# Router logits with tokens on partitions, and their place among the projection's last matmuls

## The reference, cut to what matters

```
h  = h + (y * g) @ w_o                       # layer 0's mixer; layer 1: silu(u) @ w_pw2 + b
ht = rms_norm(h, norm2_g)
gp = softmax(ht @ w_group + b_group)         # 4 groups
p_top, g_idx = top_k(gp, 1)
el = ht @ w_expert + b_expert                # 32 experts, 8 a group
el_sel = the 8 of el in the chosen group
top_l, e_idx = top_k(el_sel, 2)
gates = softmax(top_l) * p_top               # for the two experts that a token chose
h  = h + sum over experts of gate * (silu(ht @ wg) * (ht @ wu)) @ wd
```

## Time and profile before

| | us |
|---|---|
| median of 3 runs | 1217.81 |
| lowest and highest | 1216.09, 1220.73 |
| time of the profiled execution | 1218.87 |
| its span in the profile | 1217.1 |
| PE busy in that span | 1144.6 (94%) |
| DVE busy | 529.2 (43%) |
| ACT busy | 425.1 (35%) |
| mean granted clock of PE | 0.991 of 2.4 GHz |

### The profile page before, as it was taken

How to read it: one execution, slowest core, us unless ns; L and a number is a source line. 1 busy time by engine, 2 the same in 40 slices (tenths; PEclk the granted TensorE clock), 3 DMA queues, 4 the chain that set the end, 5 groups by cost and what they waited for, 6 DMA issues and landing times.

```text
span 1217.1 us, 29462 instructions
## 1 busy us (share of the span) xinstructions
PE 1144.6 (94%) x12520; PEld 627.2 (52%) x12520; DVE 529.2 (43%) x1004; ACT 425.1 (35%) x823; POOL 205.6 (17%) x234
## 2 busy tenths in 40 slices
PE   6999999999999989999998889999999999998785
PEld 5365555555555644555554445544554555554442
DVE  6756464664555510511111125899941511111125
ACT  5345354454454421321121124555443321111123
POOL 2000000000000000222222110688800112221110
PEclk9999999999999999999999999999999999999998
DMA  4017311011011258799999998126702889999996
GB/s 162 3 55 297 116 56 41 20 59 42 20 59 49 98 201 339 283 354 421 423 420 423 424 379 344 70 71 253 316 1 75 324 304 422 422 423 422 422 401 256
DMA packets 53779, 281.97 MB, mean 232 GB/s; under 512 B 14956, under 2 KB 17132, under 8 KB 36496
## 3 DMA queue, kind: packets, MB, share of 16 engines
q1 hardware_dynamic: 43952, 263.73, 54.1%
q0 software_dynamic: 9408, 16.32, 3.7%
q10 hardware_dynamic: 288, 0.03, 0.0%
HBM read 265.84 MB, written 30.41 MB: 243 GB/s over the span
## 4 chain that ended last, share of the span: by engine, by line
PE 79%; DMA 12%; DVE 3%; ACT 2%; issue 2%; SPq 1%; DVEq 0%; ACTq 0%
PE psum L1609 15%; PE psum L974 14%; PE psum L2143 9%; PE psum L2441 8%; PE psum L1790 6%; PE psum L987 6%; DMA h<-rows 5%; DMA big<-in_moe_w_gate_up_dram 4%; DMA h<-in_moe_w_gate_up_dram 4%; PE psum L941 2%; PE psum L1914 1%; PE psum L1779 1%; SPq L423 1%; PE psum L2451 1%; PE psum L2417 1%
## 5 line engine op out<-in xcount | busy, mean ns | idle before, releaser
L974 PE MATMUL psum<-big 128*64 128x256 f32 x1536 | 188.4, 388 | 24.0 <-issue 13.2
L1609 PE MATMUL psum<-big 128*128 128x512 f32 x384 | 192.8, 623 | 1.4 <-ACT big L1660 0.2
L974 PEld LDWEIGHTS psum<-big 128*64 128x64 f32 x1536 | 107.0, 138 | 92.2 <-issue 33.1
L1108 DVE SCALAR_TENSOR_TENSOR big<-psum,big 128x128 f32<-128x128 f32 x64 | 22.4, 351 | 292.2 <-ACT big L1058 292.2
L987 PE MATMUL psum<-big 128*64 128x512 f32 x512 | 121.0, 593 | 1.1 <-DMA big<-in_moe_w_down_dram 0.8
L2143 PE MATMUL psum<-big 128*128 128x512 f32 x256 | 115.6, 604 | 0.8 <-ACT big L2544 0.8
L894 POOL DMA_INDIRECT chosen<-big x60 | 59.9, 998 | 312.3 <-ACT big L1069 150.7
L1983 ACT COPY big<-psum 128x512 f32<-128x512 f32 (+1 forms) x112 | 69.1, 649 | 109.8 <-PE psum L1790 107.4
L2386 POOL TENSOR_TENSOR big<-big 128x512 f32<-128x512 f32 x76 | 96.7, 1272 | 36.0 <-ACT big L2526 25.5
L1790 PEld LDWEIGHTS psum<-big 64*64 64x64 f32 x4096 | 71.5, 134 | 49.3 <-issue 48.5
L2441 PE MATMUL psum<-big,conv_w 128*128 128x512 f32 x224 | 96.5, 592 | 0.0
(11 more groups left out here) (290 smaller groups left out, 1395.2 us busy)
## 6 DMA issues: line engine op xcount, KB each, us to landing
big<-in_moe_w_gate_up_dram SPq DMA_DIRECT2D x40, 2048.0 KB, 31.1
big<-in_moe_w_down_dram SPq DMA_DIRECT2D x64, 1024.0 KB, 27.7
conv_w<-in_moe_w_gate_up_dram SPq DMA_DIRECT2D x8, 2048.0 KB, 31.6
h<-in_moe_w_gate_up_dram SPq DMA_DIRECT2D x8, 2048.0 KB, 26.6
big<-in_moe_w_gate_up_dram SPq DMA_DIRECT2D x16, 1024.0 KB, 12.3
big<-in_rwkv_w_rkv_dram SPq DMA_DIRECT2D x24, 512.0 KB, 4.2
chosen<-h SPq DMA_DIRECT2D x8, 1024.0 KB, 12.6
conv_w<-in_conv_w_pw_dram SPq DMA_DIRECT2D x8, 1024.0 KB, 4.8
```

The costliest lines, as they stand in the source:

```text
L974: last = nc.tensor.matmul(o[half * SLOTS:(half + 1) * SLOTS, 0:F_EXP].rearrange("p (u f) -> p u f", u=2), m.xT[e // 2 % 2][:, c, (e % 2) * ...
L1609: last = nc.tensor.matmul(bank[b], m.w[:, n, c, :], x[:, c, :], start=(c == 0), stop=(c == C - 1))
```

## The change

The logits' operands change places: 128 tokens of hnT are the stationary operand and the 36 columns of the table stream past. So logits come out with tokens on partitions, and both copies and the second turning are gone. Each tile has matmuls of its own: 8 calls a tile, 32 in all, as before.

PE makes the logits of tiles 0 and 1 inside the projection, behind chunk 3 of tile 3, and turns tile 2 ahead of tile 3's last chunk. Behind the projection stay the logits of tile 2, the turning of tile 3 and the logits of tile 3. DVE chooses tiles 0 and 1 as a pair while the projection runs, then tile 2 alone and tile 3 alone; picks and token codes are made with each choice, and the two conversions of indices to float are gone. ACT codes tiles 0 and 1 early, and fills its zeros (L631) only behind all logits. `pe_stay_busy` ahead of the ranks goes from 5 matmuls to 2. PSUM banks are dealt out anew.

```diff
-        NORM_BANKS = ((6, 7), (2, 3)) * 2
+        OPENING_NORM_BANKS = ((6, 7), (2, 3)) * 2
+        NORM_BANKS = ((6, 7), (2, 3), (2, 3), (0, 1))
...
-        FLIP_BANKS = (4, 6, 5, 7)
+        LOGIT_BANK = (6, 7, 2, 0)
...
+        def pe_logits(m, pe, t):
+
+            if t == 0:
+                pe.wait_ge(m.router_scaled.sem, m.router_scaled.by(1))
             for c in range(C):
...
+                if c in (0, C // 2):
+                    pe.wait_ge(m.hnT_ready.sem, m.hnT_ready.by(2 * t + (1 if c == 0 else 2)))
+                last = nc.tensor.matmul(bank[LOGIT_BANK[t]][:, 0:N_LOGITS], m.hnT[:, c, t * P:(t + 1) * P],
+                                        m.w_route[:, c, :], start=(c == 0), stop=(c == C - 1))
+            last.then_inc(m.logits_in_psum.sem, 1)
+
+        def pe_route_last(m, pe):
+
+            pe_logits(m, pe, TT - 2)
             pe_norm_columns(m, pe, TT - 1)
-            pe_flip_logits(m, mixer, pe, 0)
-            pe_logits(m, mixer, pe, 1)
-            pe_flip_logits(m, mixer, pe, 1)
+            pe_logits(m, pe, TT - 1)
...
             for t in range(2):
                 square(t)
                 root(t)
-            columns(0)
-            square(2)
-            root(2)
-            columns(1)
-            columns(2)
-            square(3)
-            logits(0)
-            logits(1)
-            root(3)
-            columns(3)
-            logits(2)
+            for t in range(2):
+                columns(t)
+            act_low_codes(m, act, 0, 2)
+            for t in range(2, TT):
+                square(t)
+                columns(t)
+                root(t)
             act.wait_ge(m.squares.sem, m.squares.by(TT))
+            act.wait_ge(m.logits_in_psum.sem, m.logits_in_psum.by(TT))
...
+            dve_mixed(mixer, dve, 1)
+            dve_mean_square(m, dve, 1)
+            dve.wait_ge(consts_ready, 2)
+            step(nc.vector.memset(m.logits[:, :, n:], -3.0e38))
+            choose_experts(0, 2)
+            dve_mixed(mixer, dve, 2)
+            dve_mean_square(m, dve, 2)
+            dve_mixed(mixer, dve, 3)
+            choose_experts(2, 3, meanwhile=lambda: dve_mean_square(m, dve, 3))
+            choose_experts(3, 4)
...
-            pe_stay_busy(m, 5)
-            pe.wait_ge(m.route, PICKED)
+            pe_stay_busy(m, 2)
+            pe.wait_ge(m.route, PICKED[TT])
...
+        LOGITS_BEHIND = 3
...
                     for c in group:
                         add(t, c)
+                        if t == TT - 1 and c == LOGITS_BEHIND:
+                            for u in range(2):
+                                pe_logits(after, pe, u)
+                        if t == TT - 1 and c == C - 2:
+                            pe_norm_columns(after, pe, 2)
```

More of the change, by code:

```diff
@@ L561, in pe_logits @@
             for c in range(C):
[L562 to L576, removed]
@@ L669, in choose_experts @@
                 step(last)
-                for t in two:
+                for t in range(first, end):
                     last = nc.vector.max(m.gmax[:, t, :], m.logits[:, t, N_EXP:])
                 step(last)
-                for t in two:
+                for t in range(first, end):
                     last = nc.vector.max_index(m.gidx[:, t, :].bitcast(u32), m.gmax[:, t, :], m.logits[:, t, N_EXP:])
                 step(last)
-                step(nc.vector.tensor_copy(m.gidx_f[:, both], m.gidx[:, both, 0].bitcast(u32)))
@@ L685, in choose_experts @@
-                for t in two:
+                step(nc.vector.tensor_tensor(m.in_group[:, tiles, :],
+                                             group_iota[:].unsqueeze(1).broadcast_to([P, count, N_EXP]),
+                                             m.gidx[:, tiles, 0:1].bitcast(u32).broadcast_to([P, count, N_EXP]),
+                                             ALU.not_equal))
+                step(nc.vector.scalar_tensor_tensor(out=m.el[:, tiles, :], in0=m.in_group[:, tiles, :], scalar=-3.0e38,
+                                                    in1=m.logits[:, tiles, 0:N_EXP], op0=ALU.mult, op1=ALU.add))
@@ L686, in choose_experts @@
+                if meanwhile:
+                    meanwhile()
+                for t in range(first, end):
                     last = nc.vector.max(m.emax[:, t, :], m.el[:, t, :])
                 step(last)
-                for t in two:
+                for t in range(first, end):
                     last = nc.vector.max_index(m.eidx[:, t, :].bitcast(u32), m.emax[:, t, :], m.el[:, t, :])
                 step(last)
-            for pair in range(2):
-                choose_experts(pair)
-            step(nc.vector.tensor_copy(m.eidx_f, m.eidx[:, :, 0:2].bitcast(u32)))
@@ L695, in dve_route @@
-            for k in range(2):
-                last = nc.vector.tensor_tensor(m.pick[:, :, k, :], expert_iota[:].unsqueeze(1).broadcast_to([P, TT, N_EXP]),
-                                               m.eidx_f[:, :, k:k + 1].broadcast_to([P, TT, N_EXP]), ALU.is_equal)
-            step(last)
-            step(nc.vector.tensor_tensor(m.picks, m.pick[:, :, 0, :], m.pick[:, :, 1, :], ALU.add))
-            assert st.n == PICKED
-            rhs = m.route_rhs.rearrange("p (t k) n e -> p t k n e", k=2)
@@ new lines, in choose_experts @@
+                step(last)
+                step(nc.vector.tensor_tensor(m.picks[:, tiles, :], m.pick[:, tiles, 0, :], m.pick[:, tiles, 1, :], ALU.add))
+                assert st.n == PICKED[end]
+                for i in range(2):
+                    last = nc.vector.tensor_tensor(rhs[:, tiles, :, 2 + i, :], m.pick[:, tiles],
+                                                   token_high[:, i, tiles].unsqueeze(2).unsqueeze(3)
+                                                   .broadcast_to([P, count, 2, N_EXP]), ALU.mult)
@@ L2176, in pe_mix_out @@
                             pe_norm_columns(after, pe, u)
[L2177 removed]
+            pe_route_last(after, pe)
         def dve_mix(m, dve, t):
```

125 lines of the change are left out of this document (47 added, 78 removed).

## The result

| | kernel before | changed kernel |
|---|---|---|
| median, us | 1220.62 (8 runs) | 1226.96 (8 runs) |
| lowest to highest | 1216.09 to 1222.34 | 1221.96 to 1229.04 |
| ratio, 95% interval | | 1.0054, 1.0038 to 1.0070 |
| profiled execution: time, span | 1218.87, 1217.1 | 1221.96, 1220.2 |

The change costs 6.3 us by the medians and 6.6 by the ratio, where +1.5 was forecast. The profiled execution of the changed kernel is the lowest of its eight, so its trace shows less than the loss. I therefore compare pieces of the way, and use traces of several kernels.

The account below looks back on a forecast made before the run. It took the chain through PE's projection, then PE, ACT and DVE to the gather, as the bound. Layer 0 +0.3 +0.3 and layer 1 +0.05 +0.8, rounded +1.5 us, on 1217.8 gave 1219.3 us; range 1212.5 to 1226.

Parts of the forecast that it names:

- The base: Time of the kernel before that the forecast added its change to: 1217.8 us, the median of its runs.
- What bounds it: Chain through projection and routing in both layers: a shift of the first expert moves the whole layer by as much.
- The price of a pass: One pass of the new logits on PE, taken as bound by its weight load: 0.1125 us, 1.80 a tile.
- The rule of the Trainium skill: Kept as a rival at 0.12: logits' weight loads not hidden, 0.1425 us a pass, 3.8 us in all, 1223 us.
- The way to the picks: Layer 0, projection to picks: projection ends 4.5 us later, one-tile choice takes 2.1, picks come 0.45 later.
- the loads over the gather: Loads ending later lie over the first gather: +0.3 us in layer 0, +0.8 in layer 1.
- my rival on the other side: Gather waits out the loads in both layers, taking 10.7 us: 13 us in all, 1231 us; chance 0.08.
- Three fewer matmuls without use cost nothing: Two matmuls ahead of the ranks instead of five: two end near 502.6, ahead of the picks; no cost.
- the clock, a rival at 0.10: Granted clock falls in the new tail; an episode of some 3 us costs up to 1.7: 1222 to 1224 us.
- A row of mine: Profile row for layer 0: granted clock 0.50 at 445 us, after a light stretch with PE 0.40 busy.

Follow-up runs that it names:

- e5: The changed kernel with the load into h (2 MiB) held until the first gather has landed; ratio 1.0035 to the kernel before.
- e2: The changed kernel with the table's 36 columns streamed three times over (108 columns); ratio 1.0063 to the kernel before.
- e9: The changed kernel with 108 columns and the load into h held behind the first gather; 1220.79 against 1219.58 us, ratio 1.0005.
- e12: The kernel before with two instead of five matmuls without use ahead of the ranks; ratio 1.0019.
- e14: The changed kernel with the load into h held behind the first gather and four instead of two matmuls without use ahead of the ranks; ratio 1.0033.
- e1: The changed kernel measured again, unedited; 1226.11 us against 1219.18 for the kernel before, ratio 1.0048.
- e3: The changed kernel with the logits of tiles 0 and 1 behind chunk 5 of tile 3 instead of chunk 3; 1223.65 us, ratio 1.0028.
- e7: The kernel with new logit operands, but all logits and tile 2's turning behind the projection and tiles chosen in pairs; ratio 1.0031 to the kernel before.
- e10: The kernel of e9 with tile 3 turned behind chunk 5 of tile 2's logits instead of chunk 7; ranks at 26.34 us, 0.26 later.
- e13: The changed kernel with the load into h behind the first gather, one matmul without use in the copy wait and three ahead of the ranks; ratio 1.0014.
- e4: The changed kernel with a matmul without use in PE's wait for tile 3's copy and three instead of two ahead of the ranks; ratio 1.0062.
- e6: The kernel before with the store of tile 3's rows, and loads queued behind it, held until tile 3 is turned and copied; ratio 1.0023.
- e11: The kernel of e7 with 108 moving columns instead of 36; ratio 1.0022 to the kernel before.
- e8: The kernel before with the load into h held until the first gather has landed; ratio 1.0016.

## Why the prediction was wrong, point by point

**The base.** The forecast was 1217.8 + 1.5, from three runs of the kernel before. Its median over eight runs is 1220.62. So of the 7.7 us between 1219.3 and 1226.96, 2.8 are the base and the rest the change. On the old base the measured change would have ended at 1224.1, within my range; the change was still forecast four times too small.

**What bounds it: right.** Nearly all that was lost lies in the stretches from tile 3 to the first freed place. A delay there moved what is behind it by as much.

**The price of a pass: right.** 0.1125 taken, 0.109 measured. The rule of the Trainium skill ("TensorE: Matmul & The Clock Gate", Part 3, The mechanism), that loads overlap only across row groups, would have given 0.14 by my sum. It does not hold for these passes on the full array; even 108 moving columns hide under the load (0.111). The same section also lets loads into the background weight buffer go ahead, which my prediction left out; no run here shows whether that is what happens.

**The way to the picks: right.** With the clock at 1.00 (layer 0 of the changed kernel, layer 1 of e5) picks are 0.56 and 0.59 us later, against +0.45 forecast, and ranks 0.45 and 0.47. DVE's choice for one tile took 501.86 - 499.60 = 2.26 us (2.1 taken). The projection ended 4.45 later in its stretch (4.5 taken).

**The step that failed first: the loads over the gather,** taken at +0.3 and +0.8 us as "I take the lower end". How much later the loads end was forecast well: the load into h lands 4.0 and 2.6 us later in the stretch than before (5 and 2.5 forecast). But where they end was misread, and so what this does to the gather's landing: 5.47 us in layer 0 (+1.2) and, where the clock doesn't delay the issue, 6.69 in layer 1 (e2; 3.61 before). That puts e2's rows at 38.33 against 35.33, or +3.0 where all is counted. With the wait taken away, they come at 35.54 (e5) and 35.60 (e9). Between e2 and e9, which differ only in this wait, it is worth 1.0 us in layer 0 and 2.7 in layer 1, where 0.3 and 0.8 were taken, and 1.6 more in layer 1 by the clock that falls behind it. Issues of the load into h with their time to landing (layer 0 before and changed, then e2's layer 1) show the misreading:

```profile
h<-in_moe_w_gate_up_dram SPq DMA_DIRECT2D x1, 2048.0 KB, 14.3
...
h<-in_moe_w_gate_up_dram SPq DMA_DIRECT2D x1, 2048.0 KB, 14.0
...
h<-in_moe_w_gate_up_dram SPq DMA_DIRECT2D x1, 2048.0 KB, 13.0
```

I had taken the loads as through at 507, where the mean DMA share falls. Before, the last one landed at 495.49 + 14.3 = 509.8. My own 5 us more make it 514.8, behind the 513 or so at which I had the gather land, so the overlap would not have ended before the landing. In both layers of the changed kernel and of e2 the gather lands 0.3 to 0.7 us behind this load. This was my rival on the other side, with the right place and mechanism, but with a price between mine and its 13 us. The Trainium skill ("Trainium Kernel Development and Optimization", Key Constraints) has DMAs from SP's and POOL's queues run on the same 16 engines and interleave; the gather's times agree.

**The second, shown only in part: "Three fewer matmuls without use cost nothing".** In the kernel before they cost (1.0019, e12), with a wait of 2.30 us. In the changed kernel this cut can't have caused the falls ahead of the ranks: in each stretch with a star the clock fell before the first filler began, by 0.7 us (e14) or more. It may have to do with the fall behind the ranks in layer 0; that is not shown. I had looked at what fillers cover in time, and not at what they keep up.

**The third: the clock, a rival at 0.10.** I priced an episode at up to 1.7 us and asked for one. In the eight stretches of the changed kernel, e1, e3 and e5 it fell ahead of the ranks in five, and these then came 0.9 to 3.6 us later than the 26.03 of the others. In kernels with the old logits it never did, in ten stretches. The mean clock over all runs goes the same way: 0.986 in e1 and e5 and 0.984 in e7, against 0.990 before and in e9, e10 and e13. A row of mine even spoke for it. What was wrong is the argument against it: that the old tail had held 1.00 said nothing of a tail with fewer moving columns and fewer fillers.

**How the two add up.** From 1.0054 (1.0048 in e1) the two cures alone bring the ratio to 1.0063 and 1.0035, together to 1.0005. They are not additive. A gather that is issued late by the clock meets fewer loads. And behind a gather that is late by the loads, for which PE stood idle, the clock fell in e2, e4 and e6; that the wait is the reason is argued, for in e2's layer 0 PE was idle for 1.50 us and the clock held. The forecast's total of +1.5 us is close to what is left in e9, 1.2 us by the medians, but e9 is another kernel and its two stretches are only 0.8 longer, so that is partly luck.

**What stays open.** Either more columns (e2, e9, e10, e11) or fillers in both gaps (e4, e13) held the clock to the ranks in all twelve stretches; four fillers in one place (e14) did not. The passes with few columns can bring the clock down with no gap beside them (e3, e7). Whether PE's wait of 0.68 us for tile 3's copy adds to that isn't settled with one trace a kernel, nor is what brings the falls behind the ranks (e8, e11, e12), nor e3's gain.

## What to carry to other kernels

Before moving work ahead of an event, list what that event releases on every queue, and how near its last byte comes to the next latency-bound transfer; here a gather that was issued while another queue's loads filled the DMA engines landed 6.7 us after its issue (e2, layer 1) instead of 3.6 before, just behind the last of them. Read the end of loads from their landing, not from the mean DMA share. Matmuls without use ahead of a wait may have two jobs (e12), and counting the time that they cover prices only one of them; take them out only with the granted clock in view. When one cure changes nothing, look whether a second loss has taken its place before giving the first theory up, and compare stretches over several traces, as one execution can be the lucky one.

## What the runs showed that I had not expected

- Streaming 108 instead of 36 columns past 128 columns of float32 weights is nearly free: 3.56 against 3.49 us for 32 passes.
- An episode of 0.50 lasted 6.8 us in the changed kernel's layer 1, where I had priced some 3, and in e7's layer 1 from 959.5 to 973.1.
- Logits in the new operands, all of them behind the projection, reach the ranks at 25.93 us with the clock at 1.00 (e11), though PE has 7.0 us of logits there instead of 3.9: only 0.36 later than before. In these traces the new place brought no earlier ranks than the new operands alone.
